# Key norm and exponentials inside the Fourier units, modulation rows at other waits, score banks renumbered, the third output unit's split moved

## What is computed

```
h = modulate(rmsnorm(x), shift, scale)            # modulation from c @ w_ada, 6 x 1024 columns a layer
q, k, v, u_rwkv, u_fnet = split(h @ w_in)         # 2176 columns
o_attn = softmax(q k^T + mask, sink) v            # rotary on latent q and k
kk = k_r * k_k;  kk = kk * rsqrt(sum(kk*kk per head) + 1e-12)          # the key norm of the RWKV heads
log_w = -DECAY * sigmoid(w0 + tanh(wd) @ w_up);  a = sigmoid(a0 + ad @ a_up)
o_rwkv = two scans over time with exp(log_w), kk, a ...; group norm; * g
o_fnet = real part of the 2-D DFT of u_fnet
x = x + g1 * (concat(o_attn, o_rwkv, o_fnet) @ w_out)
x = x + g2 * swiglu(modulate(rmsnorm(x)))
```

## Time and profile before

| what | value |
|---|---|
| median of 3 runs | 1845.91 us (1845.08 to 1855.27) |
| the profiled execution, its own time | 1847.49 us |
| its span | 1845.5 us |
| TensorE busy | 1748.4 us (95%) |
| TensorE weight loads busy | 1634.1 us (89%) |
| VectorE busy | 1063.5 us (58%) |
| ScalarE busy | 800.8 us (43%) |
| GpSimd busy | 370.5 us (20%) |
| mean granted TensorE clock | 0.994 of full |
| moved by DMA | 161.1 MB, 87 GB/s on average |

### The profile page before, as it was taken

How to read it: one execution, slowest core, us unless ns; L and a number is a source line. 1 busy time by engine, 2 the same in 40 slices (tenths; PEclk the granted TensorE clock), 3 DMA queues, 4 the chain that set the end, 5 groups by cost and what they waited for, 6 DMA issues and landing times. The chain is left out here.

```text
span 1845.5 us, 46196 instructions
## 1 busy us (share of the span) xinstructions
PE 1748.4 (95%) x19693; PEld 1634.1 (89%) x19693; DVE 1063.5 (58%) x2328; ACT 800.8 (43%) x1723; POOL 370.5 (20%) x306
## 2 busy tenths in 40 slices
PE   7999988889999999999999998898899999999997
PEld 6999776778899999999989987777798999999997
DVE  4444677663394573838453546676519737465663
ACT  3333555542453351535433346475316525344352
POOL 3254010212302003020324421002232020201112
PEclk9999999999999999999999999999999999999999
DMA  9653600003622313241337254000021232323211
GB/s 338 204 138 110 189 5 3 6 5 107 181 69 81 91 55 107 58 113 53 98 99 200 79 164 92 5 2 7 25 69 47 69 92 81 104 61 89 83 55 58
DMA packets 215973, 161.11 MB, mean 87 GB/s; under 512 B 21968, under 2 KB 213146, under 8 KB 215770
## 3 DMA queue, kind: packets, MB, share of 16 engines
q1 hardware_dynamic: 213818, 156.13, 29.0%
q0 software_dynamic: 1952, 2.03, 0.4%
HBM read 154.99 MB, written 3.15 MB: 86 GB/s over the span
## 5 line engine op out<-in xcount | busy, mean ns | idle before, releaser
L2643 DVE SCALAR_TENSOR_TENSOR x<-PS,mod,x 128x320 f32<-128x320 f32 (+2 forms) x240 | 90.7, 433 | 296.7 <-PE PS L1071 296.7
L1106 PE MATMUL PS<-T_hi,wsplit 128*128 128x320 f32 x768 | 170.0, 309 | 0.0
L811 POOL TENSOR_TENSOR SfR<-ring,SfR 128x768 fp32r<-128x768 f32 (+1 forms) x24 | 41.2, 1715 | 582.2 <-ACT SfR L1768 582.2
L1070 PE MATMUL PS<-in_hi,win 128*128 128x320 f32 x480 | 149.7, 320 | 1.7 <-ACT mix L1836 1.0
L1071 PE MATMUL PS<-in_hi,win 128*128 128x320 f32 x480 | 144.7, 309 | 0.0
L1070 PE MATMUL PS<-hid_hi,wsplit 128*128 128x320 f32 x440 | 133.0, 310 | 0.0
L1071 PE MATMUL PS<-hid_hi,wsplit 128*128 128x320 f32 x440 | 132.5, 309 | 0.0
L1106 PEld LDWEIGHTS PS<-T_hi,wsplit 128*128 128x128 f32 x768 | 128.4, 188 | 0.0
L1106 PE MATMUL PS<-h_hi,wsplit 128*128 128x320 f32 x576 | 127.6, 309 | 0.0
L1106 PE MATMUL PS<-T_lo,wsplit 128*128 128x320 f32 x384 | 118.7, 309 | 0.0
L2079 ACT ACTIVATE wsplit<-Sf 128x512 fp32r<-128x512 f32 x96 | 59.8, 629 | 130.0 <-DVE Sf L2693 72.3
(11 more groups left out here) (536 smaller groups left out, 5413.0 us busy)
## 6 DMA issues: line engine op xcount, KB each, us to landing
ring<-in_w_ada SPq DMA_DIRECT2D x47, 1024.0 KB, 7.9
ring<-in_ffn_w_in SPq DMA_DIRECT2D x88, 512.0 KB, 5.1
ring<-in_ffn_w_out SPq DMA_DIRECT2D x16, 768.0 KB, 4.3
ring<-in_ffn_w_out SPq DMA_DIRECT2D x16, 640.0 KB, 3.9
ring<-in_w_in SPq DMA_DIRECT2D x7, 1024.0 KB, 9.3
ring<-in_w_in SPq DMA_DIRECT2D x10, 512.0 KB, 5.3
ring<-in_w_in SPq DMA_DIRECT2D x16, 256.0 KB, 5.4
ring<-in_w_out SPq DMA_DIRECT2D x16, 256.0 KB, 6.6
```

The source lines that it names most:

```text
L811: nc.gpsimd.tensor_tensor(lo, raw_w, hi, SUB).then_inc(wl_ready(), 1)
L1070: mm(lat[:, 0:TH], w, v[:, 0:TH], start=(n == 0), stop=(n == total - 1))
L1106: last = mm(bank[:, 0:TH], (w_lo if p == 1 else w_hi)[:, k, :], (v_lo if p == 2 else v_hi)[:, k, :], start=(q in (A11, A12, S1_) and k == ...
L2643: last = V.scalar_tensor_tensor(x[:, m, a:b], bank[:, at:at + b - a], mod[:, gate_at + m, s:s + 1], x[:, m, a:b], MUL, ADD)
```

## The change

In both layers:

1. **Order of items.** `fn 1` comes before `kvT`. The items `kk` and `kinv` are gone; what they computed goes to fixed places in banks 4 to 7 (`KK_SUM`, `KINV`) with semaphores of its own (`kk_ps`, `kk_root`, `kinv_ps`, `kinv_taken`).
2. **Key norm inside the Fourier units.** TensorE does both `quarters` right after `fn 0`, then the 8 products of `fn 1` that read the low input (and signals `lo_read`), 6 more, both `spread`s, and the other 10.
3. **ScalarE.** Squares, root table, both roots first; then the exponentials of the first pair (after `lo_read`), `fcopy(0)`, a one-element sigmoid, `fcopy(1)`, the `kvT` copies; and a one-element exponential after the copy of modulation row 10.
4. **VectorE.** Both key scalings follow the reciprocals; then steps 5, 11 and 12 of the first pair, the scans and steps 1 to 4 of the second, and steps 6 to 10 of the first.
5. **Modulation rows.** `ada_rows(8)` after `kvT`, `ada_rows(9)` after `w 1`, `ada_rows(10)` after `a 1`; the columns follow accordingly.
6. **Score banks.** The scores of pair m and group g go to `ps[2*g + (m + 1) % 2]`; each of the first two pairs waits for one parity only.
7. **Output stage.** The high weights of output unit 2 are made right after those of unit 1, ahead of the squares of the group norm; the two `g` items come after 4 and after 9 of the 12 early products that are left of unit 1, where they came after all of them.

Context between the changed lines is cut:

```diff
--- before.py
+++ after.py
@@ -122,9 +122,9 @@
     o += [("q", 0), ("q", 1)] + lora("w", 0) + [("q", 2), ("q", 3)]
-    o += [("k", 0), ("v", 0), ("fn", 0), ("kvT", 0), ("fn", 1)]
-    o += [("kk", 0), ("kk", 1)] + lora("w", 1) + lora("a", 0) + lora("a", 1)
-    o += [("kinv", 0), ("kinv", 1), ("ft1", 0), ("ft1", 1), ("ft1", 2)]
+    o += [("k", 0), ("v", 0), ("fn", 0), ("fn", 1), ("kvT", 0)]
+    o += lora("w", 1) + lora("a", 0) + lora("a", 1)
+    o += [("ft1", 0), ("ft1", 1), ("ft1", 2)]
     o += [("bonus", 0), ("bonus", 1), ("ft2", 0), ("ft2", 1)]
@@ -329,7 +329,8 @@
         rcol = sb("rcol", [128, 5])
-        root_table = sb("root_table", [128, 1])
+        tables_ = sb("root_table", [128, 3])
+        root_table, sigmoid_table, exp_table = (tables_[:, i:i + 1] for i in range(3))
         sink = sb("sink", [128, 8])
@@ -533,6 +534,9 @@
         kk_inv = sig("kk_inv", 2)
+        lo_read = sig("lo_read", 1)
+        kk_ps, kk_root, kinv_ps, kinv_taken = (sig("kk_ps", 1), sig("kk_root", 2), sig("kinv_ps", 2),
+                                               sig("kinv_taken", 2))
         ar_done = sig("ar_done", 2)
@@ -658,6 +662,12 @@
+        KK_SUM = [ps[4][:, 128 + QW * t:128 + QW * t + QW] for t in range(2)]
+        KINV = (ps[4], ps[5][:, 128:256]), (ps[6], ps[7][:, 0:128])
+
+        def score_bank(m, g):
+            return ps[2 * g + (m + 1) % 2]
+
         FIRST_INV = ps[5], ps[4][:, 128:256]
@@ -1071,6 +1081,7 @@
                         last.then_inc(acc_ready(), 1)
+                    return last
@@ -1189,6 +1200,21 @@
+                e.wait_ge(kk_sq.sem, kk_sq.upto(l, 2))
+                for t in range(2):
+                    last = quarters(KK_SUM[t], ones64[:, 48:80], 0, 1, rate_sq[t])
+                last.then_inc(kk_ps(), 1)
+
+                fn1 = [(k, 2) for k in range(KT)] + [(k, p) for k in range(KT) for p in range(2)]
+                unit(UNIT_OF[("fn", 1)], fn1[:KT], 3 * KT).then_inc(lo_read(), 1)
+                unit(UNIT_OF[("fn", 1)], fn1[KT:14], 3 * KT, KT)
+                e.wait_ge(swap_read.sem, swap_read.upto(l, 5))
+                e.wait_ge(mrow_sb.sem, mrow_sb.upto(l, 8))
+                e.wait_ge(kk_inv.sem, kk_inv.upto(l, 2))
+                for t in range(2):
+                    spread(*KINV[t], rate_sq[t][:, 0:QW]).then_inc(kinv_ps(), 1)
+                unit(UNIT_OF[("fn", 1)], fn1[14:], 3 * KT, 14)
+
                 lat, cx = begin(("kvT", 0))
@@ -1197,7 +1223,8 @@
                 tr(cx[:, 256:384], ckv[:, 0, :], ident).then_inc(acc_ready(), 1)
-                whole(UNIT_OF[("fn", 1)])
+                e.wait_ge(kinv_taken.sem, kinv_taken.upto(l, 2))
+                ada_rows(8, l)
@@ -1229,34 +1256,24 @@
-                for t in range(2):
-                    lat, cx = begin(("kk", t))
-                    e.wait_ge(kk_sq.sem, kk_sq.upto(l, t + 1))
-                    quarters(lat, ones64[:, 48:80], 0, 1, rate_sq[t]).then_inc(acc_ready(), 1)
                 lora_rows("w", 1)
-                lora_rows("a", 0)
-                lora_rows("a", 1)
-                e.wait_ge(swap_read.sem, swap_read.upto(l, 5))
-                ada_rows(8, l)
-                for t in range(2):
-                    lat, cx = begin(("kinv", t))
-                    e.wait_ge(kk_inv.sem, kk_inv.upto(l, t + 1))
-                    spread(lat, cx, rate_sq[t][:, 0:QW]).then_inc(acc_ready(), 1)
                 ada_cols(8, l)
                 ada_rows(9, l)
+                lora_rows("a", 0)
+                ada_cols(9, l)
+                lora_rows("a", 1)
+                ada_rows(10, l)
                 taken(e, l, ("fn", 0))
...
                 ft1(1)
-                ada_cols(9, l)
+                ada_cols(10, l)
                 ft1(2)
-                ada_rows(10, l)
                 for t in range(2):
...
                     both(lat, cx, ones64, 0, 1, bon[t]).then_inc(acc_ready(), 1)
-                ada_cols(10, l)
                 ft2(0)
@@ -1308,18 +1325,18 @@
                             src = kcT[r, :] if kind == "cache" else kt[r, 128 * t:128 * t + w]
-                            last = mm(ps[2 * (m % 2) + g][:, at:at + w], qt[r, j, 128 * b:128 * b + 128], src,
+                            last = mm(score_bank(m, g)[:, at:at + w], qt[r, j, 128 * b:128 * b + 128], src,
                                       start=True, stop=True)
...
-                    for q_ in range(2):
-                        e.wait_ge(acc_free[q_].sem, acc_free[q_].upto(l, (items_before + 1 - q_) // 2))
-
                     def scores(m):
-                        if m - 2 >= first:
+                        if m - 2 < first:
+                            q_ = (m + 1) % 2
+                            e.wait_ge(acc_free[q_].sem, acc_free[q_].upto(l, (items_before + 1 - q_) // 2))
+                        else:
                             e.wait_ge(s_sb.sem, s_sb.upto(l, 2 * (m - 1)))
@@ -1376,7 +1393,7 @@
                 late = [(k, p) for k in ROW_LATE for p in range(3)]
-                n0, n1, in_chain = 9, 6, 4
+                n0, n1, n2, n3, in_chain = 9, 6, 10, 15, 4
                 nchain = [0]
@@ -1637,10 +1654,11 @@
                     spread(lat, cx, e01[:, t, 0:QW]).then_inc(post_ready(), 1)
-                unit(NPROJ + 1, early[n1:], 3 * KT, n1)
-                for t in range(2):
-                    lat, cx = post_begin(("g", t))
-                    both(lat, cx, lora[:, 2, 128 * t:128 * t + 128], 0, 1, ush[:, 6, :]).then_inc(post_ready(), 1)
+                for a, b, t in ((n1, n2, 0), (n2, n3, 1), (n3, len(early), None)):
+                    unit(NPROJ + 1, early[a:b], 3 * KT, a)
+                    if t is not None:
+                        lat, cx = post_begin(("g", t))
+                        both(lat, cx, lora[:, 2, 128 * t:128 * t + 128], 0, 1, ush[:, 6, :]).then_inc(post_ready(), 1)
                 post_taken(e, l, ("g", 0))
@@ -1761,7 +1779,7 @@
                             e.wait_ge(acc_ready.sem, acc_ready.upto(l, ITEM_AT[("f2", m - 3, part)] + 1))
-                    elif u >= 2 and u != FFN0 + 2:
+                    elif u >= 2 and u not in (NPROJ + 2, FFN0 + 2):
                         e.wait_ge(acc_ready.sem, acc_ready.upto(l, ITEM_AT[UNITS[u - 2][0]] + 1))
@@ -1835,20 +1853,14 @@
-                e.wait_ge(cum_ready.sem, cum_ready.upto(l, 1))
-                fcopy(0)
-                free, lat, cx = ready(("kvT", 0))
-                act(vtok[:, 0:NL], lat[:, :], ACT.Copy)
-                act(vtok[:, NL:T], cx[:, 0:128], ACT.Copy)
-                act(kvout[:, :], cx[:, 128:256], ACT.Copy)
-                act(kcT[:, :], cx[:, 256:384], ACT.Copy).then_inc(free(), 1)
-
                 e.wait_ge(rot_done.sem, rot_done.upto(l, 5))
...
                 load_root_table()
-                fcopy(1)
+                e.wait_ge(kk_ps.sem, kk_ps.upto(l, 1))
+                for t in range(2):
+                    act(rate_sq[t][:, 0:QW], KK_SUM[t], ACT.Sqrt, bias=eps[:, 1:2]).then_inc(kk_root(), 1)
@@ -1881,20 +1893,27 @@
-                for t in range(2):
-                    free, lat, cx = ready(("kk", t))
-                    act(rate_sq[t][:, 0:QW], lat[:, 0:QW], ACT.Sqrt, bias=eps[:, 1:2]).then_inc(free(), 1)
+                e.wait_ge(lo_read.sem, lo_read.upto(l, 1))
+                for part in range(2):
+                    prep_exp(0, part)
+                fcopy(0)
+                act(sigmoid_table[:, :], eps[:, 0:1], ACT.Sigmoid)
+                fcopy(1)
+                free, lat, cx = ready(("kvT", 0))
+                act(vtok[:, 0:NL], lat[:, :], ACT.Copy)
+                act(vtok[:, NL:T], cx[:, 0:128], ACT.Copy)
+                act(kvout[:, :], cx[:, 128:256], ACT.Copy)
+                act(kcT[:, :], cx[:, 256:384], ACT.Copy).then_inc(free(), 1)
+                ada_rows(8, l)
                 lora_sigmoid("w", 1)
+                ada_rows(9, l)
                 lora_sigmoid("a", 0)
                 lora_sigmoid("a", 1)
-                ada_rows(8, l)
-                for part in range(2):
-                    prep_exp(0, part)
-                ada_rows(9, l)
+                ada_rows(10, l)
+                act(exp_table[:, :], eps[:, 0:1], ACT.Exp)
                 ft1_copy(0)
...
                 ft1_copy(2)
-                ada_rows(10, l)
                 for t in range(2):
@@ -2010,6 +2029,7 @@
                 weight_high(NPROJ + 1)
+                weight_high(NPROJ + 2)
                 for t in range(2):
@@ -2024,7 +2044,7 @@
                 for k in range(KT):
-                    if k + 2 < KT:
+                    if 0 < k and k + 2 < KT:
                         weight_high(NPROJ + k + 2)
@@ -2370,13 +2390,14 @@
                 def rate_inverse(t):
-                    taken(e, l, ("kk", t))
+                    e.wait_ge(kk_root.sem, kk_root.upto(l, t + 1))
                     V.reciprocal(rate_sq[t][:, 0:QW], rate_sq[t][:, 0:QW]).then_inc(kk_inv(), 1)
...
                 def rate_scale(t):
```

(20 more changed lines are left out.)

## The result

The changed kernel takes 1838.45 us (median of 7 runs, 1836.93 to 1840.32) where the kernel before took 1847.54 in the same session (7 runs). The ratio is 0.9944, with a 95% interval of 0.9931 to 0.9957: 10.3 us less by the ratio and 9.1 by the medians, where 17.2 were forecast. The median lies 9.8 us above the forecast of 1828.7 and 0.7 us above the range; of that, 1.6 us are the session, in which the kernel before was slower too (1847.54, where the forecast started from 1845.91). The profiled execution took 1839.77 us. A second measurement of the same kernel in a later session gave 0.9959 (0.9942 to 0.9975). The two intervals overlap; they say gains of 10.3 and 7.6 us, each to within about 3 us.

What follows compares the result with a forecast made beforehand. TensorE was taken as the bound, busy 1748.4 of 1845.5 us. Two layers at 4.4 + 4.2 give 17.2 us: the profiled 1847.5 becomes 1830.3, less 1.6 to the median, 1828.7; range 1825.5 to 1837.7.

Steps and rivals of the forecast that it cites:

- second place: End of the group norm, up to output unit 2: waits and low clock go, 4.2 us gained in each layer.
- The wait of 2.1 us: TensorE at output unit 2, waiting for GpSimd's low weights: goes when the split moves up, 2.1 us in each layer.
- The g items: Near output unit 1: issued earlier, they gain 0.7 us less 0.2 for a low-part wait, 0.5 us, bounds 0 and 0.9.
- the clock does not come back: Rival at output unit 2: the low clock stays without the wait, 3.2 us less gain, 1831.9 us; chance 0.12.
- The layout of the first place: End of `fn 0` to first scores: TensorE's reordered work without waits, 37.5 us against 42.0; 4.4 us gain taken per layer.
- All four waits: TensorE between `fn 0` and the scores: waits of 0.49, 0.79, 0.92 and 1.08 us, within 3.8 us per layer, go.
- the tight spot: TensorE at `a 1`, between `fn 0` and the scores: starts 0.25 us behind the first sigmoid of `a 0`.
- the one on transfers: Chunks 20 and 21 for `ada_rows(10)`: 8.6 us from issue to use, median landing 7.5; no wait, bounds 0 and 2.9 us.
- the transfers are late: Rival at `ada_rows(10)`: TensorE stands 2.9 us per layer, 4.5 with low clock, giving 1837.7 us; chance 0.17, fully or in part.
- rivals on ScalarE: Ahead of `fcopy(1)`: table switches hold ScalarE twice their row, leaving 0.7 us wait per layer, 1830.1 us; chance 0.05.
- a general slowing: Whole kernel: shifted work sets off low-clock stretches of 1.6 us in 14 places, giving 1851 us; chance 0.03.
- The prediction's sum by the page's figure: ScalarE's table switches: a load of about 1.28 us and a drain of about 1.38 each would give 1830.3 us.

Runs made afterwards that it cites:

- the bank edit: The kernel before with only the scores' banks renumbered, so that the first scores wait for the copy of `ft2 0` only: ratio 0.9986 (0.9976 to 0.9997).

## Why the prediction was right and wrong

**The forecast's direction and its second place were right.** The wait of 2.1 us and the 1.6 us of low clock behind it were sized to 0.1 us, and the one edit that removes both is worth more than half of what the change brings. The g items were put at 0.5 us and are worth 0.88. The term missed that nothing is spent again in a wait for the low part. By the traces the second place gives 4.6 us in each layer where 4.2 were forecast, 9.2 in all, and so carries nearly the whole result; the one run that measures it alone says 6.7 us (3.7 to 9.6).

**The rival "the clock does not come back" was wrong.** In the 28 layers of the 14 traces, the clock fell within 1.5 us of the start of output unit 2 in 9 of the 10 with the wait for GpSimd, and in none of the 18 without it.

**The layout of the first place was right in what it removed.** All four waits went. The roots, reciprocals and exponentials ended ahead of their use, as did the copies behind them. In layer 0 of the first trace the stretch without its two waits is 38.27 - 1.31 - 0.70 = 36.3 us, against 37.5 in the layout. The layout took `w 1` and `a 0` at 2.15 us each, about what `a 1` took in the kernel before (1089.17 to 1091.28); they take 1.29 us now (1081.54 to 1082.83, and 1085.03 to 1086.32). Since `a 0` is 0.86 us shorter, the tight spot, named and called 0.25 us to spare, comes out 0.70 short: ScalarE starts the first sigmoids of `a 0` when TensorE ends it (1086.41) and needs until 1087.25 for the two pieces that free the bank, and TensorE has only the columns, 0.39 us, to do meanwhile.

**The step that failed is the one on transfers**, "the nearest row is the first, so I take no wait, with bounds of 0 and 2.9 us". The first row was the median landing of such pairs, 7.5 us. But this pair never travels alone: before, the next one followed it by 4.7 us (the two matmul blocks of the chain start at 1091.35 and 1096.08), now by 3.5. The trace of before held only that this pair had landed within the 9.8 us between its issue and its use; it did not hold 8.6. Now the pair is complete 10.2 us after its issue (1081.67 to 1091.9) and TensorE asks for it after 7.9 (at 1089.6), not after 8.6. Measured over the four traces of kernels with this order, in both layers, the wait is 1.31, 2.43, 2.75, 2.43, 1.9, 2.5, 1.8 and 2.5 us, mean 2.2. The upper bound was good, the choice within it was not, and the low clock that comes with it was underpriced: 1.6 us were put down for it in the rival and none in the forecast, and it costs 1.3 to 1.7 where it lasts 3.4 us, and 2.1 to 2.8 where it lasts 6.8 (42.12 less its 2.43 us of wait is 39.7, against 38.27 - 1.31 = 37.0 with neither). The rival "the transfers are late" gave 1837.7; the kernel after measured 1838.45. It had a chance of 0.17.

**What neither the sum nor a rival had** is the recurrence behind the scores. Up to 34 us from the first scores the traces agree within 0.2 us, and then they part. This is TensorE's timeline of layer 0, before and after:

```profile
258.25 0.48 PE L1517 MATMUL PS<-mix 64*64 64x128 f32 x9 [0.61 <-issue]
```

```profile
257.51 0.45 PE L1534 MATMUL PS<-mix 64*64 64x128 f32 x8 [1.93 <-issue]
```

It is the same instruction, and it waits for nothing that the profile shows. In the six traces of kernels with the old order in the first place the gap ahead of it is 0.61 us or less; in the eight with the new order it is 1.38 to 2.20. From the first scores to the second part of the attention the old ones need 81.0 us in layer 0 in the mean (79.8 to 82.0), the new ones 82.2 (81.3 to 82.7); the old order has smaller gaps elsewhere in exchange (0.78 us in the second trace of before, some 6 us later). So the expectation that this was all chance is half wrong: layer 0 is about 1.2 us longer in the kernels whose earlier instructions stand in another order. Why is not shown. In layer 1 the means are 80.7 and 81.0, which is within the scatter.

**The sum, with measured terms.** The second place gives 4.6 us in each layer. In the first, the waits that went are 5.0 us in each (41.95 less 37.0, the 0.70 us of `a 1` included). Off that come 2.2 for the chunks and 1.8 for the clock (the mean of the eight layers: none in one, 1.3 to 1.7 in three, 2.1 to 2.8 in four). That leaves the first place 1.0 in each layer, and the 1.2 us of layer 0's recurrence take 0.6 in each from it. The whole is 2 x (4.6 + 0.4) = 10.0 us. Measured are 10.3 and 7.6. This sum sets the mean of eight changed layers against one quiet trace of before. The twelve layers with the old order, the 1.1 us of the bank edit given back, have a mean of 42.8 us, and the eight 40.9; taken so, the first place gains 1.9 in each layer and the whole is 11.8. The account closes to some 2 us and not better.

The rivals on ScalarE and on a general slowing did not come about. The Trainium skill (ScalarE: Activation LUTs, What ACT_TABLE_LOAD costs) has a drain of about 1.38 us beside each load. The rows after show none again: the load starts at 1075.53, where the copy before it ends, and its activation starts at 1076.83, 0.02 us behind the load's end. (The prediction's sum by the page's figure, 1830.3, comes out at 1830.4 when it is redone: two loads and drains add 2.76 us, less 1.9 of cover, in two layers, to 1828.7.)

## What to carry to other kernels

When a change brings a reader of loaded weights closer to the instruction that issues the load, count how many loads are then on the way together, and take the landing time of a crowded issue and not the median. Put the instructions that free a buffer as early as their own inputs allow: moving one block of 64 matmuls up brought 4 to 7 us here, where the whole reordering of the first place had brought 3. And time a change by its parts: one edit that takes a wait out of a dense stretch was most of this one.

## What the hardware showed that was not expected

**A wait of TensorE in a dense stretch can cost about twice its length.** The seven waits for a chunk of 1.75 us or more each came with a granted clock of 0.5 (1.2 GHz) for 3.4 or 6.8 us; the waits of 0.3 to 1.7 us for a chunk had none behind them. But the wait is not the whole cause. In two of the seven the clock fell as the wait began (at 1089.80 for the wait from 1089.59 in the first trace of after, at 1093.59 for the one from 1093.58 in layer 1 of the kernel with the g items put back), so something ahead of it must have had a part. The low clock also came without such a wait: for 3.4 us in one of the nine other layers of the new order (layer 0 with rows 10 behind `ft1 2`, at the wait of 1.19 us for a sigmoid), and for 6.8 and 10.2 us in two of the twelve layers of the old one, behind two waits for ScalarE of 0.8 and 0.9 us. The Trainium skill (TensorE: Matmul & The Clock Gate, Part 1) says that the window of activity runs free of the kernel. The traces agree in so far as the same wait is followed by a low stretch in one pass and not in another: of the ten waits for GpSimd at output unit 2, all 1.92 to 1.94 us long, one was not.

**About half of the scatter of a kernel's times goes with that clock.** Over the 162 runs of the three sessions, each against the mean of its own kernel in its session, the time moves by 1.4 us against each 0.001 of mean granted clock, with a correlation of -0.73, the square of which is 0.53. The kernel before alone ran from 1844.05 us at a clock of 0.997 to 1858.96 at 0.989. A single pair of traces can therefore mislead by several us, and layer 0 of the first trace after would have.

**A gap in untouched code follows the order of the instructions ahead of it, and its cause is open.** Beside the gaps marked "issue" the DMA records have packets on the instruction queues. After has one of 16 KB from 255.09 to 256.01 and one of 8 KB, on the other instruction queue, from 256.67 to 257.04, just ahead of the gap's end at 257.51. Before has the first from 255.44 to 256.85, and its 8 KB one only at 260.45. Whether such a fetch makes the gap was not tried: a run that moves TensorE's instructions without changing what they do could tell it.
